# A routed expert stage on one core: one program for all row counts against three programs chosen at each expert's top

## What is computed

```python
logits = xt @ w_router + b_router                 # 256 tokens, 32 experts
top_v, top_e = lax.top_k(logits, 4)               # each token goes to 4 experts
weights = softmax(top_v)
# for each expert e, its rows x:
hcat = x @ w1[e] + b1[e]                          # 1024 -> 2048
x_glu = minimum(hcat[:, ::2], 7.0)
x_lin = clip(hcat[:, 1::2], -7.0, 7.0)
act = x_glu * sigmoid(1.702 * x_glu) * (x_lin + 1.0)
y = act @ w2[e] + b2[e]                           # 1024 -> 1024
out[token] += weights[token, e] * y
```

## Time and profile before

| | us |
|---|---|
| median of 3 runs | 2190.93 |
| lowest and highest run | 2186.87, 2194.64 |
| the profiled execution's own time | 2187.02 |
| its span in the trace | 2185.2 |
| TensorE busy in the span | 1818.3 (83%) |
| VectorE, ScalarE busy | 804.7, 506.8 |
| weights of the first expert stage, 192 chunks of 2 MiB | 402.7 MB |

### The profile page before, as it was taken

How to read it: one execution, slowest core, us unless ns; L and a number is a source line. 1 busy time by engine, 2 the same in 40 slices (tenths; PEclk the granted TensorE clock), 3 DMA queues, 4 the chain that set the end, 5 groups by cost and what they waited for, 6 DMA issues and landing times. The chain is left out here.

```text
span 2185.2 us, 28329 instructions
## 1 busy us (share of the span) xinstructions
PE 1818.3 (83%) x11496; PEld 826.7 (38%) x11496; DVE 804.7 (37%) x1613; ACT 506.8 (23%) x1028; POOL 77.5 (4%) x96
## 2 busy tenths in 40 slices
PE   7899998999999998989987797699889855665556
PEld 3655445433333433424333233255544522222221
DVE  2215533333342444434443334588782200000001
ACT  2022302232331233332333233222310200000000
POOL 0000000000000000000000000084000000000000
PEclk9999999999999999989999999799999878887888
DMA  7845359789897799999999999534128299999997
GB/s 281 287 136 191 136 173 388 314 350 409 343 420 312 309 424 423 423 422 399 425 423 423 422 423 423 180 121 178 54 101 345 87 429 427 427 428 428 427 429 322
DMA packets 114820, 713.55 MB, mean 327 GB/s; under 512 B 16799, under 2 KB 21102, under 8 KB 69006
## 3 DMA queue, kind: packets, MB, share of 16 engines
q1 hardware_dynamic: 106208, 704.98, 79.1%
q10 hardware_dynamic: 8398, 5.47, 0.8%
HBM read 709.35 MB, written 1.07 MB: 325 GB/s over the span
## 5 line engine op out<-in xcount | busy, mean ns | idle before, releaser
L881 PE MATMUL ps<-ring,ar 128*32 128x512 f32 x3072 | 371.9, 624 | 44.3 <-DMA ring<-in_w 31.6
L481 PE MATMUL ps<-ar 128*128 128x128 f32 (+5 forms) x1742 | 351.4, 359 | 38.3 <-PEq L755 16.4
L488 PE MATMUL ps<-ring,ar 128*32 128x512 f32 x1184 | 196.1, 692 | 139.0 <-DMA ring<-in_w_gate 49.2
L481 PEld LDWEIGHTS ps<-ar 128*128 128x128 f32 (+2 forms) x1742 | 233.9, 200 | 159.4 <-issue 114.3
L481 PE MATMUL ps<-ring,ar 128*128 128x512 f32 (+2 forms) x592 | 247.0, 577 | 4.9 <-ACT ar L2266 2.6
L881 PEld LDWEIGHTS ps<-ring,ar 128*32 128x32 f32 x3072 | 97.8, 113 | 314.3 <-issue 264.7
L1825 DVE TENSOR_SCALAR ar<-ps 128x256 f32<-128x256 f32 x128 | 54.4, 425 | 409.7 <-PE ps L881 400.9
L893 PE MATMUL ps<-ring,ar 128*32 128x512 f32 x1536 | 173.8, 598 | 0.0
L596 PE MATMUL ps<-ring,ar 128*128 128x512 f32 x384 | 171.9, 599 | 0.0
L481 PEld LDWEIGHTS ps<-ring,ar 128*128 128x128 f32 x592 | 112.4, 191 | 132.8 <-issue 126.2
L2400 ACT ACTIVATE ar<-ps 64x512 f32<-64x512 f32 x256 | 151.5, 592 | 45.1 <-PE ps L893 30.7
(11 more groups left out here) (403 smaller groups left out, 1379.0 us busy)
## 6 DMA issues: line engine op xcount, KB each, us to landing
ring<-in_w SPq DMA_DIRECT2D x192, 2048.0 KB, 20.4
ring<-in_w_gate SPq DMA_DIRECT2D x25, 2048.0 KB, 29.1
ring<-in_w_up SPq DMA_DIRECT2D x25, 2048.0 KB, 31.4
ring<-in_w_down SPq DMA_DIRECT2D x24, 2048.0 KB, 29.8
ring<-in_w_in SPq DMA_DIRECT2D x21, 2048.0 KB, 9.0
ring<-in_w_ada SPq DMA_DIRECT2D x12, 2048.0 KB, 8.3
ar<-in_w_up SPq DMA_DIRECT2D x7, 2048.0 KB, 29.8
ar<-in_w_gate SPq DMA_DIRECT2D x7, 2048.0 KB, 29.3
```

Of the source, the lines that this page charges most:

```text
L481: ins = self.t.e.matmul(o, l, r, start=(i == 0), stop=(i == len(pairs) - 1))
L488: ins = self.t.e.matmul(b[32 * i:32 * i + 32, :], l, r, start=(k == 0), stop=(k == len(steps) - 1))
L881: ins = e.matmul(b[32 * s:32 * s + 32, :], HG[:, 2 * c + r, 32 * n:32 * n + 32], W[:, r, HALF(s)], start=False, stop=(c == 3 and r == 1))
```

## The change

Four things are changed:

- **Three programs per expert.** Ahead of each expert TensorE loads the row count of the next expert, and then branches once or twice on the count of this one: over 64 rows a program for all four passes (with the branches on 96 inside it), 33 to 64 rows a program for two passes, at most 32 rows a program for one pass. The three are laid one behind the other. The skipped counters are moved on at the top of the one-pass program (`left_out`).
- **Shared gathers and spreads.** The first 32 rows of four neighbouring experts are gathered together, once in four experts. The first 32 rows' results of two experts are spread together, two matmuls in each of the two experts that follow. Rows 33 to 128 of an expert are gathered (`gather_further`, 16 matmuls of 96 columns, inside layer 1) and spread (`spread_further`, four matmuls at the expert's end, two for each half of the columns) only in the programs that have them.
- **Buffers and order.** The transposed activations have one buffer instead of two. ScalarE evicts passes 0, 2, 3 and then 1. VectorE ends each expert with a wait for pass 1's eviction and a branch of its own.
- **Attention of the second block.** The values of unit s-3 instead of s-2 are done in step s, with one step more.

The core of the diff (renamed helpers of the second expert layer, buffers' addresses and VectorE's selections are left out):

```diff
+        def left_out(q, k):
+
+            if q.n > 0:
+                e.wait_ge(q.sem, q.n)
+            e.nop().then_inc(q.sem, k)
+            q.n += k
+
+        def expert(u, count, passes):
...
+            if passes == 1:
+                left_out(x, 7)
+                left_out(z, 4)
+            if passes < 4:
+                left_out(y, 2)
+            if u % 4 == 0 or u == HEAD:
+                t.wait_ge(s_act, act["hg", 1, u // 4, u % 4])
...
+            def spread_further():
+                for h in range(2):
+                    t.wait_ge(s_act, act["ygx", u, h])
+                    bs = [w.claim("spx", u, tb, h, lane=TL1X) for tb in range(2)]
...
             for half in range(2):
-                pe["l1", u, half] = t(layer1(b0, 0, half, True))
-                if half == 1 and u + 1 < NE:
-                    counts.append(e.value_load(flag(u + 1)))
...
-                either(t, x, count, 32, second)
+                pe["l1", u, half] = t(layer1(0, half))
+                if passes > 1:
                     if half == 0:
-                        w.claim("l1", u, n, lane=(n,))
-                    return layer1(ps("l1", u, n), n, half, False)
+                        gather_further()
+                    t.wait_ge(s_act, act["hx", u, half])
+                    if passes > 2:
+                        layer1(2, half)
+                        only(t, count, 96, lambda: layer1(3, half))
+                    px["l1", u, half] = x(layer1(1, half))
...
-            if u > 0:
-                spread1(u - 1, counts[u - 1])
+            if u > 1:
+                spread_pair(t, w, u // 2 - 1, u % 2)
...
-            pe["at", u, 0] = t(turn_act(0, (0,)))
-            if u + 1 < NE:
-                gather(t, w, 1, u + 1, TL1)
-            turn_act(1, (1,))
+            pe["at", u, 0] = t(turn_act(0, (0,), ATL))
+            if passes > 1:
+                b = w.claim("swx", u, lane=(0,))
+                t.wait_ge(s_dve, dve["selx", u])
...
+                px["at", u, 1] = x(turn_act(1, (1,), (1,)))
+            if u == HEAD - 1:
+                gather_four(t, w, 0, HEAD, 4 - HEAD)
+            elif u % 4 == 3 and u + 1 < NE:
+                gather_four(t, w, u // 4 + 1, 0, 4)
+            if u > 0 and u % 2 == 0:
+                turn_pair(t, w, u // 2)
             t.wait_ge(s_act, act["at", u, 0])
...
+            pe["l2", u, 0] = t(layer2(0, (7,)))
+            if passes > 2:
+                py["at", u, 2] = y(turn_act(2, (2, 3), (0,)))
                 t.wait_ge(s_act, act["at", u, 2])
...
+                only(t, count, 96, fourth)
+                py["l2", u] = y(layer2(2, (2,)))
+            if passes > 1:
                 t.wait_ge(s_act, act["at", u, 1])
+                px["l2", u] = x(layer2(1, (1,)))
...
+            if passes > 1:
+                spread_further()
...
+        for u in range(NE):
+            if u + 1 < NE:
+                counts.append(e.value_load(flag(u + 1)))
...
+            with e.If(counts[u] > 32):
+                with e.If(counts[u] > 64):
+                    expert(u, counts[u], 4)
...
+                with e.Else():
+                    expert(u, counts[u], 2)
...
+            with e.Else():
+                expert(u, counts[u], 1)
```

VectorE and ScalarE in the same stage:

```diff
+            vector_spread_further(v, u)
+        for tb in range(2):
+            vector_spread_pair(v, NE // 2 - 1, tb)
...
         for u in range(NE):
+            scalar_further(s, u)
             sigmoid(u, 0)
             turned_act(s, u, 0, (0,))
...
+            scalar_weights_further(s, u)
+
+            sigmoid(u, 1)
...
             for n in (2, 3):
                 sigmoid(u, n)
...
+            s.wait_ge(s_dve, dve["ac", u, 1])
+            turned_act(s, u, 1, (1,))
             turned_act(s, u, 2, (2, 3))
...
+            k = evict(u, 0)
...
+            for n in (2, 3):
+                evict(u, n)
+            evict(u, 1)
```

The attention of the second block:

```diff
-        for s in range(14):
+        for s in range(15):
             if s < 12:
                 scores(s)
-            if s >= 2:
+            if 2 <= s < 14:
                 turn_p(t, w, 2, s - 2, (0, 1), 2)
             if s < 3:
                 gate_half(t, w, 2, 11 + s)
-            if s >= 2:
-                values(s - 2)
+            if s >= 3:
+                values(s - 3)
```

More of the change, by code:

```diff
@@ L44, in __setitem__ @@
     def __setitem__(self, key, value):
-        assert (key not in self) if self.dry else (self[key] == value), key
+        assert self.get(key, value) == value and (self.dry or key in self), key
         dict.__setitem__(self, key, value)
@@ L793, in tensor_route, with gather @@
         pe["rk", m] = w.sums(b[:, 64:96], [(ones, s0), (ones, s1)])
[L795 to L805, removed]
+    def gather(t, w, u, lane):
+        b = w.claim("swt", 2, u, lane=lane)
+        t.wait_ge(s_dve, dve["sel", 2, u])
+        for tb in range(2):
+            ins = t.e.transpose(b[:, TB(tb)], SWB2[:, 0, tb, :], ident)
+        pe["swt", 2, u] = t(ins)
+        t.wait_ge(s_dve, dve["pick", 2, u])
+        t.wait_ge(s_act, act["rows", 2])
@@ L833, in tensor_moe1 @@
         x, y, z = Queue(e, s_px), Queue(e, s_py), Queue(e, s_ps)
[L835 to L847, removed]
         def biases():
             for h in range(2):
-                tensor_ada_out(t, w, 5, h, TL1)
-            b = w.claim("ct", lane=TL1)
+                tensor_ada_out(t, w, 5, h, SPL)
+            b = w.claim("ct", lane=SPL)
             for tb in range(2):
@@ L981, in tensor_dense2 @@
+        for tb in range(2):
+            spread_pair(t, w, NE // 2 - 1, tb)
     def tensor_dense2(t, w):
@@ new lines, in vector_spread, with vector_spread_pair, vector_spread_further @@
+            read["sp", 2, u, 0, tb, h] = v.mark()
+    def vector_spread_pair(v, j, tb):
+        for h in range(2):
+            v.wait_ge(s_pe, pe["spp", j, tb, h])
+            o = YV[:, tb, HALF(h)]
+            v(v.own.tensor_tensor(o, ps("spp", j, tb, h)[:, :], o, ALU.add))
+            read["spp", j, tb, h] = v.mark()
+    def vector_spread_further(v, u):
+        v.wait_ge(s_act, act["ygx", u, 1])
+        n, met = v.n, dict(v.met)
+        count = v.e.value_load(flag(u))
+        with v.e.If(count > 32):
+            for h in range(2):
+                for tb in range(2):
+                    v.wait_ge(s_ps, psp[u, tb, h])
+                    o = YV[:, tb, HALF(h)]
+                    v(v.own.tensor_tensor(o, ps("spx", u, tb, h)[:, :], o, ALU.add))
+                    read["spx", u, tb, h] = v.mark()
+        v.met = met
+        with v.e.Else():
+            v.e.wait_ge(s_dve, n)
+            v.e.nop().then_inc(s_dve, v.n - n)
@@ L1797, in vector_moe1 @@
         vector_ada(v, 5, 1)
+        v(v.own.memset(YV, 0.0))
         def biases():
@@ L2373, in scalar_moe1, with scalar_weights_further @@
+    def scalar_weights_further(s, u):
+        s.wait_ge(s_px, px["swx", u])
+        if u > 0:
+            s.wait_ge(s_ps, psp["all", u - 1])
+        s(s.own.activation(SWTX, ps("swx", u)[:, 0:256], ACT.Copy))
+        s(s.own.activation(SWT3, ps("swx", u)[0:64, 256:512], ACT.Copy))
+        read["swx", u] = s.mark()
     def scalar_moe1(s):
@@ L2528, in values @@
                 act["branch", 2, 1] = k
-        for k in range(14):
-            if k >= 3:
-                values(k - 3)
-            if k >= 2:
+        for k in range(15):
+            if k >= 4:
+                values(k - 4)
+            if 2 <= k < 14:
                 scalar_turned_p(s, 2, k - 2, 4)
```

432 lines of the change are left out of this document (241 added, 191 removed).

## The result

The changed kernel takes **2402.2 us** (median of 4 runs, 2399.8 to 2406.2) against 2188.9 of the kernel before in the same job: 1.097 times, 95% interval 1.0944 to 1.1001. I had forecast 2210, with 2160 to 2258 as the range. The side was right, the loss about eleven times as large as I thought (213 us for 19). One run of a later kernel, e5, took 8597.7 us where its other nine took 2178.5 to 2193.3; it stands in that kernel's median and not in its ratio.

The account below looks back on a forecast made before the run. Up to expert 9's release TensorE was taken as the bound, then what the weight stream can't hide. Terms 26.8 + 5 - 6 - 7 = +19 us on 2187.0, with 3.9 for the median, gave 2210 us; range 2160 to 2258.

Parts of the forecast that it names:

- terms for jumps: TensorE's jumps over programs: 44.8 us up to expert 9's release, 5 us more in later experts.
- The failed step, first: One-pass experts: the four-pass round of VectorE and ScalarE, about 17 us, stays just under the forecast's one-pass time.
- The failed step, second: Each far jump on TensorE costs 3.0 us idle plus 1.7 us slow restart, 4.7 us; nine up to expert 9's release.
- the 3.5 to 6 us of my forecast: Price of a far jump on TensorE in the main case, giving 2198 to 2228 us; chance 0.45.
- rival B: Far jumps on TensorE are dearer, following each other behind three-pass experts: at 7 us each 2241 us; chance 0.20.
- the later stalls: After expert 9, jumps are hidden by the weight stream except around experts 18, 27 and 28: 5 us, between 0 and 15.
- The pieces without jumps: TensorE's experts 0 to 9 without jumps: one pass 15.1 us, two 36.75, three 49.8, expert 0 33.7; 338.2 in all.
- The start: First block's expert stage starts 2.5 us earlier, at 389.2, as the first gather has 64 columns instead of 128.
- The end of the stage: End of the expert stage: no needless wait, fewer spread matmuls, VectorE's branch before its last adds: -6 us (0 to -8).
- The attention: Second block's attention: with values a step later the wait for ScalarE's copy goes, -7 us (-3 to -8).
- rival C: Expert stage and attention cancel, or the stream hides TensorE and only attention gains: 2187 to 2195 us; chance 0.10.

Follow-up runs that it names:

- e5: Changed kernel with programs fixed by this input's counts (no TensorE branches, no fourth pass), further spread on banks 7 and 4, third turned copy in bank 3: 2185.4 us.
- e7: e5 with the first gather made for four experts at once (128 columns) instead of two and two (64 and 64): 2181.8 us.
- e10: Changed kernel, programs still chosen by counts, with further spread on banks 7 and 4, third turned copy in bank 3, first gather for four experts: 2321.7 us.
- e6: e5 with the count loaded and a four-pass program behind a never-true condition at each of the 32 expert tops: 2311.8 us.
- e9: e6 with a second never-true condition over a second program behind the first at each of the 32 tops: 2536.8 us.
- e4: Kernel before with only the change's attention loop, the values done a step later: 2180.9 us.

## Why the prediction was right in sign and wrong in size

**From 2210 to 2402.** Without its terms for jumps (44.8 and 5 us) my sum gives 2160.2. e7, which has no jumps, takes 2181.8: the pieces were 21.6 us too short. e10 is e7 with the choice at run time and takes 139.9 us more, where I had 49.8: the jumps were 90.1 us too cheap. The changed kernel takes 80.5 us more than e10: the two bank waits and the narrow first gather, to which I gave no cost. Together 192.2 us. So the largest error is the price and number of bare jumps, and the bank, though its wait is the longest in the profile, comes second, since a part of it covered jumps.

**What the 217 us are made of.** From e5 (2185.4) to the changed kernel (2402.2) the idle time ahead of line 891 rises from 2.7 to 252.4 us (162.7 for the bank, 81.0 for the sequencer, 8.7 issue), and lines 891 and 898 are busy 483.5 instead of 423.1 us, the lower clock behind the gaps (79.6 and 403.9 in the changed kernel). That is 249.7 + 60.4 = 310.1. Off go the waits for weights, 69.4 and 10.8, and 11.4 of line 920's: 218.5, against 216.9 measured.

**The failed step, first.** "VectorE and ScalarE still do four passes; their round is ... about 17 us. That is under the forecast's one-pass time (below), but just." The 17 us were about right, but the sentence supposes that the round overlaps the next expert's layer 1. It can't: VectorE's branch at the end of the round is what frees bank 0. Expert 3 of the changed kernel starts at 545.28, VectorE's first instruction on it stands at 556.92 (11.6 us), ScalarE's last eviction ends at 572.97 (16.1) and the next expert starts at 573.73 (0.8). That is 28.5 us in a row; the later ones take 27 to 28 us (expert 14, with other work in it, 36.4), where I had 19 to 22. I had costed which instructions each program runs and read the bank list only where a program uses it; a claim that the short program never makes held up the next expert.

**The failed step, second.** "I take 3.0 idle + 1.7 slow = 4.7 us." By e6 a single jump costs 4.4 + 2.0 = 6.4, by e9 a second one 7.0. The idle part was wrong, the slow part nearly right, and the price is above the 3.5 to 6 us of my forecast and close to rival B's 7, to which I gave 0.20. The gaps of 10.3 to 10.5 us behind experts 2 and 4 are B's too ("two or three follow each other"). The other half of the error is my count of where they are bare: "One-pass experts then need about 20 us, below the 29.7 of the stream, so later jumps are hidden". Once a one-pass expert needs 27 us and a three-pass one 67 (expert 18: 1123.11 to 1190.37), nothing later is hidden (no wait for weights is left in the list of the kernel after), and the 5 us for the later stalls became 86, bank waits included.

**The pieces without jumps**, from e7: one-pass experts 14.8 (expert 5; predicted 15.1) and 18.4 with a gather (predicted 18.4). Three passes 51.9 to 53.0 instead of 49.8, two passes 42.9 (expert 6) instead of 36.75, and expert 0 39.0 instead of 33.7. The timeline of expert 6 in e7 has the difference:

```profile
595.05 3.78 PE L929 MATMUL ps<-ar 128*128 128x96 f32 x32 [2.42 <-ACT ar L2519]
...
615.20 0.66 PE L920 MATMUL ps<-ar 128*128 128x128 f32 x2 [2.38 <-DVE ar L1931]
...
616.22 8.15 PE L910 MATMUL ps<-ring,ar 128*32 128x512 f32 x64
625.73 1.98 PE L940 MATMUL ps<-ar 128*128 128x512 f32 x4 [1.36 <-ACT ar L2519]
628.59 1.96 PE L940 MATMUL ps<-ar 128*128 128x512 f32 x4 [0.88 <-DVE ar L1854]
```

The wait of line 920 (2.38; predicted 2.2 to 2.6) and the eviction's (1.36; predicted 0.9 to 1.1) are the ones I named. Missing were the wait of the 96-column gather for the evictions of the expert before (2.42 here, 0.33 at expert 2), the 0.88 between the halves of the spread, the slower layer 2 (8.15 for 7.07), and the gather itself: 3.78 instead of the 3.0 that I took; the end of my bounds, 3.84, was right. Together the first matmuls of experts 0 and 10 lie 359.8 us apart in e7, while I had 338.2 for experts 0 to 9. So even without a jump expert 10 starts at 754.5, 13.6 us later than before, not 18.0 earlier.

**The start** was put 2.5 us earlier and is 9.0 later. The gather begins 1.9 us later (385.65 for 383.78); it is no cheaper and leaves the clock low (11.7 us from it to the first matmul in e5, against 8.8 in e7 and 7.9 before); and at the first top TensorE idles 3.2 us more, which none of the static kernels without a jump does. **The end of the stage** was put at -6 and gives nothing. In e7 ScalarE's evictions end at 1390.93, but TensorE then still has the pair's spread and VectorE its adds:

```profile
1391.69 1.49 DVE L1841 TENSOR_TENSOR ar<-ps,ar 128x512 f32<-128x512 f32 x2 [6.80 <-DVEq L1859]
...
1396.25 0.69 DVE L1841 TENSOR_TENSOR ar<-ps,ar 128x512 f32<-128x512 f32 x1 [1.02 <-PE ps L483]
1399.74 1.22 DVE L1952 TENSOR_TENSOR ar<-ar 128x1024 f32<-128x1024 f32 x1 [2.80 <-issue]
```

VectorE comes to the next stage at 1399.74; before it was 1399.83, with nearly the same idle sequencer. **The attention** was right: -7 predicted, -7.8 in e4, with steps of 2.72 us where I had 2.85.

**What the change could have brought at best.** With the jumps, both bank waits and the narrow gather gone, e7 reaches 2181.8 us, no less than the 2180.9 of the kernel before with the attention alone. The next stage's first matmul stands at 1407.21 in e7, at 1407.30 in the kernel before and at 1408.18 with the attention alone. The second stretch of e7:

```profile
741.00:1180.00 439.00, 353.23 (x2478) 116.88 (x2482) 177.42 (x374) 157.92 (x326) 0.00 (x0) 0.91 0.99 416
```

TensorE has 40 us less to do there than before (353 for 393), and the stream moves the same 416 to 419 GB/s at a DMA share of 0.99. The gathers and spreads that were shared had been free there: they stood under the weights. My rival C had this in its last sentence; it holds for e7, and with the jumps in place it doesn't.

**What stays open.** Whether the end of the three-pass program is one jump to TensorE or two, and with it whether each far jump has the same price: I varied their number and order, never the length jumped over or the work ahead alone. The share of `value_load` in the 6.4 us is open too, and so is why a narrow gather leaves the clock low.

## What to carry to other kernels

Where several programs share one table of marks, the shortest path waits for what only the longest does: for each bank that the next step claims first, look up its holder in the program that the table was taken from, and when that holder's mark is set on the path that really runs. A jump over a whole program cost 6.4 to 7.0 us on TensorE here (4.0 where waits for weights took up a part), so it has to save more than that, and more than what the stream would have hidden anyway. Before splitting a program to spare instructions, ask in which stretch the engine is the bound: here it was some 350 of 1016 us, and there the two- and three-pass experts, which the split made longer, take most of the time.

## What was not expected of the hardware

- With 128 x 128 weights the number of moving columns hardly mattered up to 128: 32 records take 3.68 us with 64 columns, 3.81 with 96 and 3.84 with 128, and 64 columns took up to 7.09 where the clock was at its lower level. (The Trainium skill, TensorE: Matmul & The Clock Gate, Back-to-back issue gap, says that in a stream of loads and matmuls both set the spacing; the rows agree: in the 128-column gather of expert 3 of the kernel after the 32 loads are busy 3.65 of the 3.84 us.)
- The narrow first gather ran at the lower clock level (0.50 granted) and so did the 64 records behind it, 3.64 us; behind the 128-column gather they took 1.96 (1.00 granted).
- A far jump brings two instruction packets (63 for 32, then 65 for 32 more), and the second of two in a row costs 7.0 us where the first costs 6.4.
- While TensorE waited behind expert 2, the weights stopped as well, since no slot came free: 423 GB/s from 535 to 540 us, 52 from 540 to 545 and 7 from 545 to 550. TensorE's idle time became the stream's own pause.
